# Scores of the eight 96-feature heads: each product over 96 rows split into one over 64 rows and one over 32, in the same bank

## The reference, cut to what matters

```
def mla_attention(c_q, c_kv, k_rope, pos, q_norm, w_uq, kv_norm, w_ukv):
    q = (rms_norm_2(c_q, q_norm) @ w_uq).reshape(B, S, H, MLA_NOPE + MLA_ROPE)      # H = 8, 64 + 32
    q = concatenate([q[..., :MLA_NOPE], apply_rope(q[..., MLA_NOPE:], pos)], axis=-1)
    kv = (rms_norm_2(c_kv, kv_norm) @ w_ukv).reshape(B, S, H, MLA_NOPE + MLA_V)
    k_nope, v = kv[..., :MLA_NOPE], kv[..., MLA_NOPE:]
    k_r = apply_rope(k_rope[:, :, None, :], pos)
    k = concatenate([k_nope, broadcast_to(k_r, (B, S, H, MLA_ROPE))], axis=-1)
    # for each block of 128 queries
        s = einsum('bqhd,bkhd->bhqk', qb, k) * 96 ** -0.5      # then causal mask
        p = softmax(s, axis=-1)
        out = einsum('bhqk,bkhd->bqhd', p, v)
```

## Time and profile before

| what | value |
|---|---|
| median of 3 runs | 974.15 us |
| the profiled execution | 973.86 us |
| its span, first to last instruction | 972.0 us |
| TensorE matmul busy | 964.7 us, 99% |
| TensorE weight load busy | 794.7 us, 82% |
| VectorE busy | 742.9 us, 76% |
| ScalarE busy | 506.5 us, 52% |
| GpSimdE busy | 65.7 us, 7% |
| mean granted clock of TensorE | 0.998 |
| scores of the eight 96-feature heads | between 749.6 and 766.7 us of the span |

### The profile page before, as it was taken

How to read it: one execution, slowest core, us unless ns; L and a number is a source line. 1 busy time by engine, 2 the same in 40 slices (tenths; PEclk the granted TensorE clock), 3 DMA queues, 4 the chain that set the end, 5 groups by cost and what they waited for, 6 DMA issues and landing times.

```text
span 972.0 us, 12800 instructions
## 1 busy us (share of the span) xinstructions
PE 964.7 (99%) x4548; PEld 794.7 (82%) x4548; DVE 742.9 (76%) x1268; ACT 506.5 (52%) x682; POOL 65.7 (7%) x97
## 2 busy tenths in 40 slices
PE   9999999999999999999999999999999999999997
PEld 6877888888888888888888888888887788888886
DVE  6898885478668887885778878786758877878784
ACT  7645555644464444444774444445648664444442
POOL 4101000020020000000120000000203020000000
PEclk9999999999999999999999999999999999999999
DMA  9765455434566555654565656544654255656531
GB/s 347 264 198 158 160 174 180 140 130 173 173 215 214 187 202 185 204 180 168 175 229 185 205 178 206 183 147 137 220 175 151 87 174 176 213 175 211 177 129 44
DMA packets 98724, 175.67 MB, mean 181 GB/s; under 512 B 5920, under 2 KB 54128, under 8 KB 98672
## 3 DMA queue, kind: packets, MB, share of 16 engines
q1 hardware_dynamic: 97024, 171.53, 52.6%
q0 software_dynamic: 1344, 3.19, 1.2%
q10 hardware_dynamic: 304, 0.27, 0.1%
HBM read 173.91 MB, written 1.05 MB: 180 GB/s over the span
## 4 chain that ended last, share of the span: by engine, by line
PE 94%; DVE 4%; POOL 1%; issue 1%; ACT 0%; POOLq 0%; ACTq 0%
PE bank L518 84%; PE bank L532 3%; DVE qaT L1606 1%; DVE w_lo L1540 1%; PE bank L577 1%; PE bank L576 1%; PE bank L809 1%; DVE kaT L1606 1%; PE bank L588 1%; PE bank L948 1%; PE bank L648 0%; POOL g_rows L2210 0%; PE bank L814 0%; PE bank L1010 0%; POOL rs L2194 0%
## 5 line engine op out<-in xcount | busy, mean ns | idle before, releaser
L518 PE MATMUL bank<-w_hi,hA 128*128 128x512 f32 (+1 forms) x1720 | 537.6, 390 | 0.2 <-DVE w_lo L1540 0.2
L1540 DVE TENSOR_TENSOR w_lo<-raw,w_hi 128x2048 fp32r<-128x2048 f32 (+1 forms) x159 | 358.0, 2260 | 94.8 <-ACT w_hi L1085 93.9
L1085 ACT ACTIVATE w_hi<-raw 128x2048 fp32r<-128x2048 f32 (+1 forms) x162 | 306.1, 1894 | 169.3 <-PE bank L518 163.9
L518 PEld LDWEIGHTS bank<-w_hi,hA 128*128 128x128 f32 x1720 | 321.4, 188 | 67.0 <-issue 1.4
L518 PE MATMUL bank<-w_lo,hA 128*128 128x512 f32 (+1 forms) x860 | 328.1, 388 | 0.0
L518 PEld LDWEIGHTS bank<-w_lo,hA 128*128 128x128 f32 x860 | 161.6, 188 | 32.2
L1901 DVE STREAM_TRANSPOSE act_T<-act_f 32x128 f32<-32x128 f32 x288 | 87.1, 302 | 3.7
L518 PE MATMUL bank<-w_hi,fT_hi 128*128 128x512 f32 x232 | 71.8, 391 | 0.0
L518 PE MATMUL bank<-w_hi,fT_lo 128*128 128x512 f32 x232 | 71.5, 389 | 0.0
L518 PE MATMUL bank<-w_lo,fT_hi 128*128 128x512 f32 x232 | 71.5, 389 | 0.0
L1353 ACT ACTIVATE act_r<-bank,rs 128x256 f32<-128x256 f32 x44 | 20.9, 475 | 58.5 <-PE bank L518 56.7
(11 more groups left out here) (296 smaller groups left out, 905.7 us busy)
## 6 DMA issues: line engine op xcount, KB each, us to landing
raw<-in_w_in SPq DMA_DIRECT2D x74, 512.0 KB, 4.5
raw<-in_w_ff SPq DMA_DIRECT2D x64, 512.0 KB, 4.2
raw<-in_ffn_w_gate SPq DMA_DIRECT2D x44, 512.0 KB, 3.9
raw<-in_ffn_w_up SPq DMA_DIRECT2D x44, 512.0 KB, 4.8
raw<-in_ffn_w_down SPq DMA_DIRECT2D x44, 512.0 KB, 4.0
raw<-in_w_out SPq DMA_DIRECT2D x16, 512.0 KB, 4.3
raw<-in_w_branch_diff SPq DMA_DIRECT2D x8, 512.0 KB, 4.0
raw<-in_w_branch_ret SPq DMA_DIRECT2D x8, 512.0 KB, 4.2
```

The costliest lines, as they stand in the source:

```text
L518: mm = pe.matmul(o, a, w, start=first and t == 0 and m < len(outs), stop=last and t == n - 1 and m >= len(todo) - len(outs))
L1085: act.activation(w_hi[u % HI_SLOTS][:, 0:w], raw[u % RAW_SLOTS][:, 0:w], ACT.Copy).then_inc(hi_ready, 1)
L1540: vec.tensor_tensor(w_lo[u % RAW_SLOTS][:, 0:w], raw[u % RAW_SLOTS][:, 0:w], w_hi[u % HI_SLOTS][:, 0:w].bitcast(f32), ALU.subtract).then_i ...
```

## The change

In `head_scores`, the branch of the "l" heads no longer calls `scores`. It has its own loop over the same two ranges of queries and keys, and makes two products in each: one over rows 0 to 63 (the features without rotation) that starts the sum in the bank, and one over rows 64 to 95 (the rotated ones) that adds to it. `NOPE` is 64 and `MQ` is 96. The wait ahead is the same, and the semaphore that tells VectorE that the scores are there is raised by the last of the four products. Nothing else is changed.

```
             else:
-                scores(("l", h), qT, kT, h)
+                m, b = SM["l", h], score(("l", h))
+                pe.wait_ge(score_out, m - 1)
+                for c, tb, n in ((slice(0, P), 0, P), (slice(P, 384), 1, SEQ)):
+                    rows = slice(tb * P, tb * P + P)
+                    pe.matmul(b[:, c], qT[0:NOPE, h, rows], kT[0:NOPE, h, 0:n], start=True, stop=False, skip_group_check=True)
+                    mm = pe.matmul(b[:, c], qT[NOPE:MQ, h, rows], kT[NOPE:MQ, h, 0:n], start=False, stop=True,
+                                   skip_group_check=True)
+                mm.then_inc(score_done, 1)
```

## The result

The changed kernel takes 991.87 us (median of 6 runs, 988.55 to 993.36) against 974.18 us before (6 runs, 973.94 to 974.86). The ratio is 1.0179, with a 95% interval from 1.0169 to 1.0190. The forecast was 985.7 us and the range ended at 988.3, so the direction was right and 6 us were missing. The runs also scatter by 4.8 us, where those of before scatter by 0.9.

The account below looks back on a forecast made before the run. TensorE's matmul stream was taken to bound the kernel. Second streaming 5.24 us plus changes of division 6.3 us made 11.5, and 974.15 + 11.5 = 985.7 us; range 979.8 to 988.3 us.

Parts of the forecast that it names:

- What bounds the kernel: TensorE's matmul stream, busy 964.7 of 972.0 us; what it grows by, the kernel grows by.
- The second streaming: Scores of the "l" heads: each head streams its columns twice, 8 x 0.655 = 5.24 us more on TensorE.
- 0.195 us for a change of division: Scores and group borders: 0.09 emptying plus 0.105 uncovered load per change, 33 changes, 6.44 us before a deduction.
- The 0.15 taken off for the transposes: After three groups, transposes' load is only partly bare, 0.06 in place of 0.105; second term becomes 6.3 us.
- The upper bound of 0.27: Per change of division, if a load begins only when the last pass has ended; total 988.3 us.
- the lower of 0.09: Per change of division, the emptying alone with the load hidden; total 982.4 us.
- Semaphores and order: Score waits, VectorE's later work and DMA order: costed at nothing, covered by TensorE's own longer stream.
- The clock: Granted clock falling to the lower level in the scores: streaming another 10.5 us, 996 us; chance 0.03.
- a clock below 1.00: Sign that the prediction is wrong: the granted clock in the second group's scores falling below full.
- Rival 1: Scores: 64 and 32 rows count as one division, no emptying between, one behind the other; 980.2 us, chance 0.08.
- Rival 2: Scores: each head's 64-row and 32-row products run side by side, 0.9 us more, 975.1 us; chance 0.09.
- the counter-argument: Against side-by-side products: the trace's pair has equal tiles and two banks; here sizes differ and both write one bank.

Follow-up runs that it names:

- the kernel with heads apart: Against the changed kernel: half of the products with w_out put between the two heads of a group, 37 changes of division; 987.39 us.
- the run with two banks: Against the changed kernel: products reordered so one head's 64-row product stands beside the other head's 32-row product in another bank; 989.36 us.

## Why the prediction was right or wrong, point by point

**What bounds the kernel.** Right. TensorE's matmuls wait for nothing new, and the whole difference is in their stream.

**The second streaming, 5.24 us.** Right; 5.4 measured by itself, and 15.97 for three more (990.13 - 974.16) against 15.7.

**0.195 us for a change of division, also between 64 and 32 rows, and 33 of them.** Right. The step that no row of before showed has the price of its neighbours: a product over 128 columns takes 0.42 us and one over 256 takes 0.62, which is 0.2 over streaming. Five orders with 5, 9, 17, 32 and 33 changes fit the same price to 0.5 us: the first four in their runs at full clock, the last with the clock's loss taken off. The 0.15 taken off for the transposes is 3 x 0.045 = 0.135 by its own rows, which changes nothing in the forecast. The upper bound of 0.27 was not needed, and the lower of 0.09 is excluded.

**Semaphores and order, nothing.** Right. With less cover it need not stay so: the kernel with heads apart has a new wait of 1.05 us.

**The clock.** This is the step that failed: the sum has the clock at full, so its term for the clock is nothing. The prediction said of a fallen clock: "This stretch, with the changes of division that it has already, ran at 1.00", gave it 0.03, and priced it at 10.5 us. All three were wrong in a way that can be named. The stretch of before held seven changes of division, into and out of the products with 64 output partitions (749.58, 758.55, 759.36, 764.26, 765.07, 769.97 and 770.78), and all its scores used 96 rows; it was no evidence for 33 more with 64 rows and 32 in use. And the price was taken as if the scores alone ran slow, all of them. It is 6.3 to 6.8 us in the profiled run, from about 3 to 8 over the six runs, and in the profiled run most of it is paid by the transposes and full products behind the scores, which the change did not touch. The "10.5 of the 17 us" also sets the streaming of the changed kernel against the stretch of the kernel before; in the changed kernel the scores reach from 749.72 to 774.27, 24.6 us. The prediction did name a clock below 1.00 as a sign that it was wrong, and that sign came. Of the measured 17.7 us between the medians (991.87 - 974.18) the forecast's 11.5 leaves 6.2, and the two runs next to the median have a mean clock of 0.991, where the table takes off 7.2.

**The rivals.** Rival 1, one division for 64 and 32 rows, would have given 980.2 and blocks without gaps; the first timeline rules it out. Rival 2, side by side, is out by the same rows, and the run with two banks says that unequal tiles are enough to keep them apart. The common bank, which the counter-argument had put beside that, is neither needed nor ruled out. That the Trainium skill ("TensorEngine Tiling (Array Packing)", Key Properties) has a change of tiling mode drain TensorE agrees with the 0.2 us at each step from 64 to 32 rows. The rule of the Trainium skill that products over few rows in distinct row groups run concurrently ("TensorE: Matmul & The Clock Gate", "Why this matters for your kernels") agrees with the 64-feature heads, whose tiles are of one size (0.86 us for both); for 64 rows beside 32 it did not come true here (3.96 us for 2.62 of streaming).

**What stays open.** Why TensorE's clock falls is shown only in part. Fewer rows at work lower it, more changes of division over the same rows go with more low stretches, and with full products between the heads it stayed up. How these combine was not worked out. Rows and gaps may be two sides of one quantity, such as how much of the array is at work over the stretch; no run sets the one against the other. With four runs to most kernels, "one of four" and "three of four" are orders, not rates. Nor was a kernel found that beats the one before: the best of those that make the full sum in two products, by two heads, is still 6.9 us slower (980.83 against 973.96), and 5.2 us of that is the second streaming.

## What to carry to other kernels

A float32 product over 96 rows took the same time here as one over 64 or 32, so splitting it by features doubles its cost unless the parts run side by side. In this kernel only tiles of one size did. Each step between divisions of the array cost TensorE 0.2 us, so order products by division first and by head second. And after pricing such a stretch, ask what it does to TensorE's clock: few rows, with many changes of division or in a long stretch, brought it to half, and most of the bill came in the dense products behind, where nobody had changed anything.

## What the runs showed of the hardware that was not expected

TensorE's granted clock falls to 0.50 although its matmuls are busy all the time by the profile. Thirty-two passes over 32 rows, back to back, ended at the lower level (7.63 us for 5.24 of streaming), while the same passes over 96 rows ran at full clock in all four runs. Until now I had read a full row of busy time as safety for the clock; it is not. The level is one of two in every stretch shown, 1.00 or 0.50, up to rounding at the edges.

The second thing is how exactly the rest adds up: with the clock full, five kernels came out within 0.3 us of sums made from two prices, 0.655 us for a head's streaming and 0.195 for a change of division (979.4, 980.3, 982.6, 981.0 and 977.2 forecast; 979.4, 980.1, 982.7, 980.8 and 977.3 measured, where 982.7 is the one run of four that kept the full clock and the others are medians).
